# Attention over a prompt: tiles early and late in turn, all keys prepared first

## The reference

```
s_c = q  . ck * SCALE                  # 63 compressed blocks
p_c = masked_softmax(s_c, cmp_end <= pos);     o_c = p_c @ cv
s_s = qr . k_sel * SCALE               # selected blocks: here all 16, so all keys up to pos
p_s = masked_softmax(s_s, kpos <= pos);        o_s = p_s @ v_sel
s_w = qr . k_win * SCALE               # the last 512 positions and the own
p_w = masked_softmax(s_w, window mask);        o_w = p_w @ v_win
o   = g[0]*o_c + g[1]*o_s + g[2]*o_w   # gates per head
```

## Time and profile before

| | |
|---|---|
| median of 3 runs | 2115.14 us (2114.45 to 2116.53) |
| profiled execution | 2109.37 us, span 2107.7 us |
| mean granted TensorE clock | 0.925 |
| attention of the prompt, first maximum to last add | 490.99 to 842.90 us of the span |
| busy over the whole span | PE 88%, PEld 75%, DVE 49%, ACT 40%, POOL 9% |

### The profile page before, as it was taken

The page is one execution under the profiler, slowest core; times in us unless marked ns, Lnnn a source line. Parts: engine busy times, 40 slices in busy tenths (PEclk is TensorE's granted clock), DMA queues, the critical chain, the costliest instruction groups (busy, mean ns, idle before and its releaser), DMA issues. The chain is left out here.

```text
span 2107.7 us, 26787 instructions
## 1 busy us (share of the span) xinstructions
PE 1850.3 (88%) x9832; PEld 1584.7 (75%) x9832; DVE 1040.5 (49%) x1928; ACT 836.4 (40%) x1702; POOL 185.7 (9%) x334
## 2 busy tenths in 40 slices
PE   5996885767879898768978997999999999999997
PEld 4896873446767776556856886899998999989996
DVE  3532244555777877445434433543445544454444
ACT  4310322224666665423115442443334433344343
POOL 0001102103333332001000000000000000000000
PEclk8998896886899999888988999899999999999999
DMA  5513503320000000424010410334334334344441
GB/s 187 195 38 88 137 1 100 92 61 8 1 1 1 1 1 1 129 91 165 1 61 1 140 41 30 98 127 143 123 119 150 120 125 143 131 150 160 136 143 65
DMA packets 110649, 184.56 MB, mean 88 GB/s; under 512 B 19248, under 2 KB 80112, under 8 KB 110471
## 3 DMA queue, kind: packets, MB, share of 16 engines
q1 hardware_dynamic: 90495, 156.32, 21.7%
q0 software_dynamic: 8080, 25.26, 3.7%
q10 hardware_dynamic: 11968, 1.58, 0.6%
HBM read 174.64 MB, written 12.73 MB: 89 GB/s over the span
## 5 line engine op out<-in xcount | busy, mean ns | idle before, releaser
L2401 DVE TENSOR_TENSOR mlp_dn_lo<-top_w_out_raw,mlp_dn_hi 128x1024 fp32r<-128x1024 f32 x96 | 117.6, 1225 | 299.5 <-ACT mlp_dn_hi L2324 299.5
L2241 PE MATMUL mlp_psU<-mlp_xT_hi,mlp_up_hi 128*128 128x384 f32 (+1 forms) x768 | 253.9, 331 | 5.3 <-DVE mlp_up_lo L2395 5.3
L2241 PE MATMUL mlp_psU<-mlp_xT_lo,mlp_up_hi 128*128 128x384 f32 (+1 forms) x768 | 252.2, 328 | 0.0
L2241 PE MATMUL mlp_psU<-mlp_xT_hi,mlp_up_lo 128*128 128x384 f32 (+1 forms) x768 | 252.0, 328 | 0.0
L2324 ACT CAST mlp_dn_hi<-top_w_out_raw 128x1024 fp32r<-128x1024 f32 x96 | 100.6, 1048 | 267.4 <-PE mlp_acc L2263 187.4
L2263 PE MATMUL mlp_acc<-mlp_dn_hi,mlp_h_hi 128*128 128x512 f32 x512 | 199.4, 389 | 0.0
L2263 PE MATMUL mlp_acc<-mlp_dn_hi,mlp_h_lo 128*128 128x512 f32 x512 | 199.2, 389 | 0.0
L2263 PE MATMUL mlp_acc<-mlp_dn_lo,mlp_h_hi 128*128 128x512 f32 x512 | 199.2, 389 | 0.0
L2241 PEld LDWEIGHTS mlp_psU<-mlp_xT_hi,mlp_up_hi 128*128 128x128 f32 x768 | 145.1, 189 | 9.4 <-issue 3.3
L2241 PEld LDWEIGHTS mlp_psU<-mlp_xT_lo,mlp_up_hi 128*128 128x128 f32 x768 | 145.1, 189 | 3.1
L2241 PEld LDWEIGHTS mlp_psU<-mlp_xT_hi,mlp_up_lo 128*128 128x128 f32 x768 | 145.0, 189 | 0.0
(11 more groups left out here) (399 smaller groups left out, 3973.2 us busy)
## 6 DMA issues: line engine op xcount, KB each, us to landing
top_w_out_raw<-in_w_up SPq DMA_DIRECT2D x48, 1024.0 KB
top_w_out_raw<-in_w_down SPq DMA_DIRECT2D x48, 1024.0 KB
cross_mem<-in_cache_mem_kv SPq DMA_DIRECT2D x8, 1024.0 KB, 5.1
qkv_w_raw<-in_w_in SPq DMA_DIRECT2D x8, 652.0 KB, 6.3
mem_w_raw<-in_w_mkv SPq DMA_DIRECT2D x8, 512.0 KB, 4.8
cmp_raw<-in_cache_cmp_kv SPq DMA_DIRECT2D x32, 128.0 KB
cmp_raw<-in_cache_cmp_kv POOLq DMA_DIRECT2D x32, 128.0 KB, 6.1
smp_sel<-in_cache_sel_kv SPq DMA_DIRECT2D x32, 128.0 KB
```

The source lines that it names most:

```text
L2241: m = nc.tensor.matmul(psU[n % 2][:, 0:w], a[:, u % 2, c, :], b[:, g % 2, c, 0:w], start=(c == 0 and n_pass == 0), stop=(c == KC - 1 and n ...
L2401: nc.vector.tensor_tensor(dn_lo[:, u % 2], dn_raw[:, k, a, :], dn_hi[:, u % 2].bitcast(F32), ALU.subtract).then_inc(s_dl, 1)
```

## The change

The units alternate: tile 0 of group 0, tile 7 of group 1, tile 1 of group 0, tile 6 of group 1, and so on to tile 7 of group 0 and tile 0 of group 1. All eight key tiles are prepared by the end of the first round, tile 0's ahead of it and the others at every second place in it. The queries of a unit are prepared during the round before (two preparations for the four heads of its group), those of units 0 and 1 ahead of the first round and at its end. The doubled keys get two buffers, which lie in a part of the probabilities not yet in use. `places` now looks at the unit before to tell when a place is free. Core of the diff (semaphore counts that only follow the new order left out):

```
-    units = [(i, g) for i in range(n_tiles) for g in range(NG)]
+    units = [(u // 2, 0) if u % 2 == 0 else (n_tiles - 1 - u // 2, 1) for u in range(NG * n_tiles)]
...
-        for s in range(3):
-            yield "prep", (0, s)
+        yield "keys", (0, 0)
+        for v in range(2):
+            yield "queries", (0, v)
         for u in range(len(units) + 1):
             blocks = list(range(len(key_blocks(u - 1)))) if u else []
-            prep = []
-            if u < len(units):
-                i, g = units[u]
-                prep = [(i, 3), (i, 4)] if g == 0 else [(i + 1, s) for s in range(3) if i + 1 < n_tiles]
...
+            prep = {}
+            if u == 0:
+                for i in range(1, n_tiles):
+                    prep[2 * i - 2] = ("keys", (i, 0))
+                prep[13], prep[14] = [("queries", (1, v)) for v in range(2)]
+            elif u + 1 < len(units):
+                prep[1], prep[5] = [("queries", (u + 1, v)) for v in range(2)]
...
-                    if prep and k == 1:
-                        yield "prep", prep.pop(0)
+                    if 4 * hh + k in prep:
+                        yield prep[4 * hh + k]
...
-        k_dup = ph.sb("k_dup", [P, 2, NG, 2, HD])
+        k_dup = prob[:, 2 * HPG - 2:2 * HPG, 0:4 * P].rearrange("p e (b g u d) -> p e b g u d", b=2, g=NG, u=2)
...
-            a = (512 * (n % 2), 2) if (i + 1) * P <= 512 else (0, 1)
+            def narrow(i):
+                return (i + 1) * P <= 512, cols_of(i)[1] + NCH <= 512
+
+            before = narrow(units[(n - 1) // HPG][0]) if n else (True, True)
+            a = (512 * (n % 2), 2 if before[0] else 1) if narrow(i)[0] else (0, 1)
...
                 def double_keys(i):
-                    if i:
-                        pool.wait_ge(s_qt, 5 * (i - 1) + 1)
+                    if i >= 2:
+                        pool.wait_ge(s_qt, prep_no["keys", (i - 2, 0)] + 1)
...
-                def double_queries(i):
+                def double_queries(u):
+                    i, g = units[u]
+                    if u >= 2:
+                        pool.wait_ge(s_qt, prep_no["queries", (u - 2, 1)] + 1)
+                    hs = slice(HPG * g, HPG * g + HPG)
...
                 double_keys(0)
                 double_queries(0)
+                for i in range(1, n_tiles):
+                    double_keys(i)
+                double_queries(1)
                 for kind, arg in steps():
-                    if kind == "prep" and arg[1] == 1 and arg[0] + 1 < n_tiles:
-                        double_keys(arg[0] + 1)
-                    if kind == "prep" and arg[1] == 4 and arg[0] + 1 < n_tiles:
+                    if kind == "scale" and arg[1] == 0 and 1 <= arg[0] and arg[0] + 1 < len(units):
                         double_queries(arg[0] + 1)
...
                     elif kind == "sel scores":
-                        pe.wait_ge(s_ql, 5 * i + (3 if g == 0 else 5))
+                        pe.wait_ge(s_ql, prep_no["queries", (u, 1)] + 1)
+                        if hh == 0:
+                            pe.wait_ge(s_ql, prep_no["keys", (i, 0)] + 1)
```

More of the change, by code:

```diff
@@ L1111, in places @@
         def places(i, n):
-            a = (512 * (n % 2), 2) if (i + 1) * P <= 512 else (0, 1)
+            def narrow(i):
+                return (i + 1) * P <= 512, cols_of(i)[1] + NCH <= 512
+            before = narrow(units[(n - 1) // HPG][0]) if n else (True, True)
+            a = (512 * (n % 2), 2 if before[0] else 1) if narrow(i)[0] else (0, 1)
             nwin = cols_of(i)[1]
-            b = (512 * (n % 2), 512 * (n % 2) + nwin, 2) if nwin + NCH <= 512 else (0, WB * P, 1)
+            b = (512 * (n % 2), 512 * (n % 2) + nwin, 2 if before[1] else 1) if narrow(i)[1] else (0, WB * P, 1)
             return *a, *b
@@ L1143, in prompt_attention @@
         s_dve = ph.sem("vector_chain")
-        def prep_no(arg):
-            return 5 * arg[0] + arg[1]
+        prep_no = {}
+        for kind, arg in steps():
+            if kind in ("keys", "queries"):
+                prep_no[kind, arg] = len(prep_no)
         bank, drained = {}, []
         for kind, arg in steps():
-            if kind in ("block", "prep"):
+            if kind in ("block", "keys", "queries"):
                 bank[kind, arg] = psT[len(drained) % len(psT)]
-                drained.append((s_tl, base[arg[0]] + arg[1] + 1) if kind == "block" else (s_ql, prep_no(arg) + 1))
+                drained.append((s_tl, base[arg[0]] + arg[1] + 1) if kind == "block" else (s_ql, prep_no[kind, arg] + 1))
         with nc.Block() as block:
@@ L1163, in double_keys @@
                 def double_keys(i):
[L1164 to L1165 removed]
+                    if i >= 2:
+                        pool.wait_ge(s_qt, prep_no["keys", (i - 2, 0)] + 1)
                     k = yq[:, i, C_KS:C_KS + 2 * KVW].rearrange("p (b u g d) -> p b u g d", b=2, u=2, g=NG)[:, :, 0]
                     for b in range(2):
[L1168 removed]
+                        m = nc.gpsimd.tensor_copy(k_dup[:, i % 2, b], k[:, b].unsqueeze(2).broadcast_to([P, NG, 2, HD]))
@@ L1228, in _ @@
                         fill += 1
-                    if kind == "prep":
-                        i, s = arg
-                        pe.wait_ge(s_kd if s == 0 else s_qd, i + 1)
+                    if kind in ("keys", "queries"):
+                        pe.wait_ge(s_kd if kind == "keys" else s_qd, arg[0] + 1)
                         for x in range(4):
-                            src = k_dup[:, x // 2, x % 2] if s == 0 else q_dup[:, (s - 1) % 2, 4 * ((s - 1) // 2) + x]
+                            if kind == "keys":
+                                src = k_dup[:, arg[0] % 2, x // 2, x % 2]
+                            else:
+                                src = q_dup[:, arg[1], HPG * units[arg[0]][1] + x]
                             m = nc.tensor.transpose(bank[kind, arg][:, x, :], src.rearrange("p a b -> p (a b)"), ident[:, :])
@@ L1302, in _ @@
                 for kind, arg in steps():
[L1303 to L1307, removed]
+                    if kind in ("keys", "queries"):
+                        act.wait_ge(s_qt, prep_no[kind, arg] + 1)
+                        if kind == "keys":
+                            i = arg[0]
                             dst = k_hi[:, :, :, i * P:(i + 1) * P]
@@ L1312, in _ @@
                         else:
-                            dst = qS[:, (s - 1) % 2, 4 * ((s - 1) // 2):4 * ((s - 1) // 2) + 4, :]
+                            g = units[arg[0]][1]
+                            dst = qS[:, arg[1], HPG * g:HPG * g + HPG, :]
                             nc.scalar.mul(dst, bank[kind, arg][:, :, :], SCALE).then_inc(s_qh, 1)
@@ L1358, in _ @@
                 for kind, arg in steps():
[L1359 to L1363, removed]
+                    if kind in ("keys", "queries"):
+                        dve.wait_ge(s_qh, prep_no[kind, arg] + 1)
+                        if kind == "keys":
+                            i = arg[0]
                             dve.wait_ge(s_vh, i + 1)
@@ L1372, in _ @@
                         else:
-                            q = qS[HD:P, (s - 1) % 2, 4 * ((s - 1) // 2):4 * ((s - 1) // 2) + 4, :]
+                            g = units[arg[0]][1]
+                            q = qS[HD:P, arg[1], HPG * g:HPG * g + HPG, :]
                             nc.vector.scalar_tensor_tensor(q, bank[kind, arg][HD:P, :, :], SCALE, q.bitcast(F32), ALU.mult,
```

12 lines of the change are left out of this document (5 added, 7 removed).

## The result

The changed kernel takes 2140.3 us (median of 4 runs, 2138.24 to 2143.74) against 2114.8 for the kernel before on the same chip: ratio 1.0123 with a 95% interval of 1.0105 to 1.0140. That is 25.5 us slower, and outside the predicted range. The profiled execution has a span of 2136.6 us, 28.9 more than before. The stage from the first maximum to the last add takes 374.93 us (495.95 to 870.88) instead of 351.91: **+23.0**. What follows the stage is 0.9 longer. The other 5.0 lie ahead of its first maximum and are scatter: from the load of the masks, with which the stage begins, to the first maximum it is 9.90 before and 9.89 after, and in the experiments that leave the code ahead of the stage alone the first maximum lies anywhere from 490.2 to 499.5. One execution, in the experiment busy, took 3090.56 us at a mean granted clock of 0.551 and is left out of its time.

A forecast was written before the change was run, and what follows sets the result against it. Heads were taken as bound by a ring through in-order VectorE, ScalarE and TensorE, no engine full. Tail -12.4, first unit +8.3 and later units +2.4 sum to -1.7: 2107.7 us profiled, median 2113, no change; range 2102 to 2126.

The forecast's parts named there:

- The tail: After the last unit: 3 blocks in place of 14, 18.18 us down to 5.8, so -12.4; ends -9.9 and -14.
- Unit 0: First round, now with seven key tiles: heads 6.7 + 3.6 + 3.6 + 6.5 = 20.4 us against 12.10, +8.3.
- all in the ring: Middle heads of the first unit: VectorE's own 1.28 us, twice 1.02 for keys, 0.3 between instructions, making 3.6.
- the bound: First unit: seven key tiles each losing 0.41 us to GpSimd's port lock would add 2.9; none counted.
- The price of k1: Block at a head's second place, its hi copy holding the exponential: 0.5 us, ends 0 and 1.0; nothing in full late heads.
- the late units: Five units with scores of tiles 5 to 7 beside few blocks: 107.3 us by the list; ends 1.5 each either way.
- The price of k0: Block at a head's first place: a lo part ahead of the maximum, 0.61 us.
- The doubling of the queries: GpSimd doubles queries after the last scaling, covered some 2 us by drain and first maximum; ends 0 and 0.5 a unit.
- The keys out of the later units: Seven later units lose a key tile at 0.9 us each, -6.3, inside the unit prices.
- The second rival: Late heads stay at 5.5 us whatever their blocks, window scores waiting for one PSUM place: 2124 us, chance 0.20.
- The first rival: TensorE's clock stays up and many-block units reach its floor of some 18.5 us instead of 20: 2104 us, chance 0.35.
- the early units: Five units with early-tile scores beside 12 to 14 blocks: 100.2 us by the list; ends 1.5 each either way.

The follow-up runs named there:

- busy: Changed kernel plus three 512-column TensorE products nobody reads ahead of waits for score places in the five late-score, few-block units: 2129.14 us, ratio 1.0083 to the kernel before.
- keys_k01: Changed kernel with the first round's seven key tiles at the first and second places of each head, not first and third: 2133.43 us, 1.0103 to the kernel before.
- k1_late: Changed kernel with the second-place block issued behind exponential and window maximum in units of tiles 5 to 7 beside at most 7 blocks: 2126.26 us, 1.0063 to kernel before.
- early_q: Changed kernel with queries doubled on GpSimd one unit earlier, at the third head's scale: 2130.73 us, ratio 1.0079 to the kernel before.
- old_fix: Changed kernel with the old unit order, queries doubled a unit earlier, first-round keys at first and second places of each head: 2118.75 us, 1.0027 to kernel before.
- the three edits: Changed kernel with late second-place block, queries doubled a unit earlier and first-round keys at first and second places, together: 2122.63 us, 1.0049 to the kernel before.

## Why the prediction was wrong

The prediction's own sign of failure was met: a stage outside 340 to 363 us, and it is 374.9. Five of its terms failed, the price of a block at k1 in late units most.

- **The tail** was right: -13.0 against -12.4. The sum has a slip of 0.4 here: it takes the tail from 824.72 and the units up to 825.15, so 0.43 of a drain counts twice, in favour of the change. The forecast does not hang on it.
- **Unit 0** failed in the terms for its middle heads, 5.0 and not 3.6, and for its first head, 8.1 and not 6.7. The forecast put "all in the ring" on VectorE and let ScalarE's copies run beside it; the order within a place denies that at k2. keys_k01 gives back 4.4 in the unit and brings it to 19.8, with a first head of 6.6 and middle heads of 3.5 and 3.7, so the rest of the working stands. GpSimd's copies of the keys were not over early, as the forecast had it: with two buffers they run until 505.96, each pair behind TensorE's transposes. Counted at nothing, GpSimd's work cost next to nothing even so: VectorE's value part took 0.56, 0.50 and 0.49 us in three places of unit 0 instead of 0.42, the first beside a GpSimd copy, the others beside a scaling. That is 0.29 against the 2.9 of the bound. The Trainium skill, SBUF — State Buffer, "SBUF: two separate sides", says that whichever of the two starts first gets the shared pair of ports for its whole instruction. The three slow value parts, each begun during a GpSimd instruction, agree with it; a fourth, begun at 507.47 during a scaling, took 0.43 and does not.
- **The price of k1** failed in the late units. "I take 0.5, ends 0 and 1.0", but the upper end was the row itself, and the cover of a full late head was taken to last. That it comes from TensorE kept busy and fast by many blocks is argued, not shown; that a late head with few blocks is without it is shown. The hi copy holds the exponential for up to 2.4, and the clock of a late unit falls as low as 0.81. k1_late removes 8.4 of the 12.8, about 5.5 of it order and 3 the clock.
- **The price of k0**, 0.61 for a lo part, left out the way there. In the last late unit the next maximum starts 2.2 after its scores at the half clock, and in k1_late, at full clock, 1.8 after them (1.2 after VectorE is free); it waits for transposes, hi copy and lo part of the k0 block in succession.
- **The doubling of the queries** failed. "Cover: the drain and the first maximum" overlooked that a first head of an early tile has that ring full of blocks, and that TensorE's in-order stop delays them all. Counted at nothing, it cost 5.7 in the first heads and 6.5 in the stage (early_q).
- **The keys out of the later units** were counted at -6.3, 0.9 each. In old_fix the six rounds from unit 2 on gain 2.1 by it, some 0.35 each, and unit 1 gets 1.8 longer, so next to nothing is left. That the keys lay partly in time that another engine set fits this, but no run isolates it.
- **The second rival's** number for the late units, 119.5, was the nearest, which is luck, as its mechanism was not: late heads behind a unit's first take 4.5 to 5.0 us with a k2 block alone, and those with a k1 block 5.4 to 9.3. The sign that was to decide for it, a late head without a k3 block at over 5.0, could not tell it from the price of k1. The first rival fell: no early unit came below 19, and the mean clock is 0.919, before 0.925.

The range failed in one more way. Unit 0 at +12.1 lies inside its own ends (+5 to +13), and so do the early units at +6.8 (five times 1.5); only the late ones, at +12.8, lie outside. But the range took one rival at a time, so it had no room for three parts at their upper ends at once.

With the three edits the stage is 357.9, the forecast 350.7 by the table; what is left lies in the late units (+4.8, part of it the price of k0) and the early ones (+3.8). In part it is the clock: the 9.30 head, untouched by the edit, takes 7.85 and 6.62 in keys_k01 and early_q, at mean clocks of 0.80 and 0.99, and the one of 6.21 takes 8.53 in early_q. Which head the half clock falls on was not controlled, and the rest of the first heads of early tiles stays open.

## What to carry to other kernels

Where work is interleaved into a ring of in-order engines, price each inserted piece by what stands directly before and behind it on each engine, and check that the cover it had in the old mix (here TensorE busy with blocks) still exists in the new one. Work gathered ahead of a loop is not saved: here each key gave back 0.35 us where it left and cost more where it went. Where the parts of a forecast have ends, ask what the sum is if several of them lie at the same end. And look for the cheap part of a large change: here one short unit moved to the end, with queries doubled early, gave 0.2%, and the whole reordering with its three collisions mended gave nothing.

## What the runs showed of the hardware

The unit of tile 7 beside 5 blocks, with TensorE busy 19.58 of its 26.74 us, has a mean granted clock of 0.81 after the change; in k1_late, busy 16.62 of 23.05, the same unit has 0.92. Unit 0, busy 17.63 of 24.21, has 0.50. With three additional products ahead of the waits the unit of tile 7 has 0.99 and the other four late units 0.94 to 1.00. The products were worth 5.3 us of the stage where a block's copy stands ahead of the exponential, and 1.8 where it does not.
